# Attention units inside a projection: scores of unit u+2 and context of unit u in one insertion, at uneven pairs

## The chip, the cores and the metric

The kernel runs on one core of a Trainium2 chip. The metric is the device time of one execution in microseconds (us). Kernel before: 1154.33 us, the median of 3 runs (1154.14 to 1155.83).

## What is computed

Two layers of a decoder trunk on 256 tokens of width 1024, all in float32:

```python
for l in range(DEPTH):                      # DEPTH = 2
    x = x + 0.5 * swiglu(rmsnorm(x, ...), ...)          # 1024 -> 2816 -> 1024
    h = rmsnorm(x, mix_norm[l])
    proj = h @ w_in                         # q, k, v of A, B, C and 3 x 1024 gate columns
    ya = moba_attention(qa, ka, va) @ w_branch_a                 # A: causal, 4 heads of 64
    yb = sliding_window_sink_attention(qb, kb, vb, sinks) @ w_branch_b   # B: window 128, sink
    oc = differential_attention(q1, q2, k1, k2, vc, lam)         # (A1 - lam * A2) V, 4 heads
    yc = from_heads(rmsnorm(oc, diff_subln) * (1 - lam_init)) @ w_branch_c
    x = x + (sigmoid(g0) * ya + sigmoid(g1) * yb + sigmoid(g2) * yc) @ w_out
    x = x + 0.5 * swiglu(rmsnorm(x, ...), ...)
```

Every q and k head is normalised and rotated (rope) first. With 256 tokens A is plain causal attention.

## The kernel before

**Engines.** Each engine runs a list of its own, in the order in which the Python code emits it, and they meet through counting semaphores (`sem[...]`). TensorE (PE) multiplies. A float32 weight is split into two parts: ScalarE (ACT) writes `w_high` (`high`, L846), VectorE (DVE) writes the rest `w_low` (`low`, L1089). A product is three passes (`three_passes`, L489, L492, L493). Weights pass through a ring of 6 slots in units called pairs: one pair is 12 matmuls of 128x512, and ACT and DVE prepare pair m+5 or so while PE runs pair m.

**The mixing stage** of a layer is the projection `h @ w_in` in 46 pairs (`PROJ`: QC, KC, VC, QA, VA with four pairs each, KBC with two, then six gate chunks with four each), then 8 pairs for the three branch products and 8 for `w_out`. The attention is put in between these pairs. It consists of 8 units (`UNITS`: 0 to 3 of kind C, 4 and 5 of A, 6 and 7 of B), two heads each, and a unit u takes, in this order:

- S: its scores on PE (`scores`, L693, L694, banks 4 and 5), then `mask_scores` on DVE (L1261 to L1274) and `exps` on ACT (L994), then `normalise` on DVE (L1289 to L1305)
- T: the probabilities are turned on PE (`turn_probs`, L708; three transposes for C, six for A and B), and copied by ACT (`copy_probs`, L1003)
- C: the context product on PE (`context`, L718 to L725), read by ACT (`read_context`, L1011, L1014) and for A and B also by DVE (`context_low`, L1312), which alone counts `context_read` there

In the kernel before, unit u has S ahead of pair 16+3u, T four pairs behind S and C five behind S. The rotated q and k are turned by PE in four rope turns (`rope_turn`, L678; ahead of pairs 10, 15, 25, 31) and copied by ACT (`copy_rope`, L985). The four contexts of C are squared (`SUBLN_AT`, ACT L1043), summed (DVE L1319), turned into a scale (POOL) and scaled (`subln`, DVE L1328), and then turned by PE ahead of pair 37 (`O_TURN`, L503). Turned rope blocks, probabilities, contexts and these last blocks share banks 6 and 7, which is why PE waits for their readers.

What belongs to PE's insertion ahead of pair p stands in the lists of ACT and DVE at step m = p + 5 (RING - 1), and exps and normalise at p + 6, each ahead of the `high` or `low` of that step. `read_proj` (L961) empties a chunk's bank at the step six behind its last pair. Four gate chunks are copied and get their sigmoid later, at steps 44 to 47 (`SIGMOID_AT`, L1050); all others at once. Behind the projection the B branch is multiplied first, then A (`a_quarter`, banks 0 to 3), then C.

Of the kernel before, what the change touches and what calls it, by code (L numbers as in the profile page):

```python
# [41 lines left out]
P = 128  # L42
# [17 lines left out]
PROJ = [(QC, 512), (KC, 512), (VC, 512), (QA, 512), (VA, 512), (KBC, 256)] + [(GATES + 512 * g, 512) for g in range(6)]  # L60
# [36 lines left out]

TURN_AFTER, CONTEXT_AFTER = 4, 5

# [8 lines left out]
    "proj_done": len(PROJ), "proj_read": len(PROJ), "head_squares": 5, "head_totals": 6, "heads_scaled": 6, "tables_ready": 1, "rope_done": 5,  # L108
# [35 lines left out]
def build(nc, a):  # L144
    ctx = ExitStack()
    with ctx:
# [75 lines left out]
        GROUP_BANKS = {ST_FFN1: (4, 5, 6, 7), ST_MIX: (2, 3, 2, 3), ST_O: (6, 7, 6, 7), ST_MERGED: (2, 3, 2, 3), ST_FFN2: (4, 5, 6, 7)}  # L222
# [19 lines left out]
        def a_quarter(half, cols):  # L242
            return bank[half + 2 * cols]
# [23 lines left out]
        def _(sp):  # L267
# [79 lines left out]
            for layer in range(DEPTH):  # L347
# [10 lines left out]
                fill(layer, n, local_heads(a["w_branch_b"], layer))  # L358
                n += 1
                for w, k0 in ((a["w_branch_a"], 0), (a["w_branch_c"], 0), (a["w_branch_c"], 2),  # L360
                              (a["w_out"], 0), (a["w_out"], 2), (a["w_out"], 4), (a["w_out"], 6)):
# [13 lines left out]
        ROPE_CHUNKS = {0: 1, 1: 2, 3: 3, 4: 4, 5: 5}  # L375
        SQUARES_AT = {0: 9, 1: 13, 3: 21, 4: 28, 5: 32}
        ROPE_AT = {0: 10, 1: 14, 3: 22, 4: 29, 5: 33}
        SIGMOID_AT = {6: 44, 7: 45, 8: 46, 9: 47}
        SUBLN_AT = 35
        LAMBDA_AT = 15  # L380
        MERGE_B_AT, MERGE_A_AT, MERGE_C_AT, MERGED_AT = 52, 54, 55, (56, 60)

        ROPE_HEADS = {0: (0, 8, 0, [(0, 8, True)]), 1: (1, 8, 8, [(1, 8, False)]), 3: (0, 8, 16, [(2, 4, True), (3, 4, False)]),
                      4: (1, 4, 24, [(4, 4, True)]), 5: (0, 2, 28, [(5, 2, False)])}
# [14 lines left out]
        def _(pool):  # L399
# [47 lines left out]
            def scale_context(layer):  # L447

                total, v, r = (small[:, k, 0:HALVES * 4] for k in (4, 2, 7))
                pool.wait_ge(sem["head_totals"], value("head_totals", layer, 6))  # L450
# [34 lines left out]
        def _(pe):  # L485
# [181 lines left out]
            def rope_turn(layer, n):  # L667

                first, count, _ = ROPE_TURNS[n]
                pe.wait_ge(sem["rope_done"], value("rope_done", layer, (1, 2, 3, 5)[n]))  # L670
# [11 lines left out]
            def scores(layer, u):  # L682

                kind, qb, kb, _ = UNITS[u]
# [12 lines left out]
            def turn_probs(layer, u):  # L697
# [7 lines left out]
                pe.wait_ge(sem["rope_copied"], value("rope_copied", layer, sum(pos < UNITS[u][3] + TURN_AFTER for _, _, pos in ROPE_TURNS)))  # L705
                for t in range(1 if kind == "C" else 2):
                    for b in range(3):
                        last = nc.tensor.transpose(bank[6 + t][:, b * P:(b + 1) * P], probs_of[u % 2][:, t, b * P:(b + 1) * P], ident[:, :])  # L708
                last.then_inc(sem["probs_turned"], 1)

            def context(layer, u):

                kind = UNITS[u][0]
                pe.wait_ge(sem["probs_copied"], value("probs_copied", layer, u + 1))
                if kind == "C":
                    out, c0 = bank[7], 384 + u * P
# [4 lines left out]
                else:  # L721
                    for half, queries, keys in ((0, slice(0, S), slice(0, S)), (1, slice(P, S), slice(S, S + P))):
                        for t in range(2):
                            c0 = (2 * (u - 4) + t) * DH if kind == "A" else 256 + t * DH
                            last = nc.tensor.matmul(bank[6][t * DH:t * DH + DH, queries], values[:, half, c0:c0 + DH], probsT[:, t, keys],  # L725
# [3 lines left out]
            def mixing(layer):  # L729
                chunk, j = 0, 0  # L730
                for m in range(PROJ_PAIRS):
# [20 lines left out]
                    if m == O_TURN:  # L752
                        pe.wait_ge(sem["subln_ready"], value("subln_ready", layer, 1))
                        pe.wait_ge(sem["context_read"], value("context_read", layer, 6))
# [11 lines left out]
            def branches(layer):  # L766
                p = BRANCH0

                pe.wait_ge(sem["scores_masked"], value("scores_masked", layer, 8))
                pe.wait_ge(sem["context_read"], value("context_read", layer, 8))  # L770
                last_pairs(layer, p, oT_high, oT_low, 2, True, release=1)

                pe.wait_ge(sem["proj_read"], value("proj_read", layer, len(PROJ)))
                last_pairs(layer, p + 2, oT_high, oT_low, 0, True, release=2, banks=a_quarter)
# [58 lines left out]
        def _(act):  # L833
# [113 lines left out]
            def read_proj(layer, chunk):  # L947
# [5 lines left out]
                done = {3: 1, 4: 2, 5: 3}.get(chunk)  # L953
# [3 lines left out]
                for half in range(HALVES):  # L957
                    source, scale = bank[2 * (chunk % 2) + half], norm_scale[:, half:half + 1]
                    if chunk >= 6:
                        c0 = 512 * (chunk - 6)  # L960
# [5 lines left out]
                             5: [(qk_raw[0], 0, 0, 128), (values, 256, 128, 128)]}[chunk]  # L966
# [4 lines left out]
            def head_squares(layer, chunk):  # L971
# [3 lines left out]
                if chunk:  # L975
                    act.wait_ge(sem["rope_done"], value("rope_done", layer, {1: 1, 3: 2, 4: 3, 5: 4}[chunk]))
# [23 lines left out]
            def copy_probs(layer, u):  # L1000
                act.wait_ge(sem["probs_turned"], value("probs_turned", layer, u + 1))
                for t in range(1 if UNITS[u][0] == "C" else 2):
                    last = act.activation(probsT[:, t], bank[6 + t][:, 0:3 * P], ACT.Copy)  # L1003
# [449 lines left out]
```

## Time and profile before

| | |
|---|---|
| median of 3 runs | 1154.33 us |
| the profiled execution | 1154.52 us, its span 1152.7 us |
| PE busy | 1141.2 us (99%) |
| DVE busy | 781.1 us (68%) |
| ACT busy | 639.1 us (55%) |
| granted TensorE clock | 1.0 throughout |

How to read it: the span runs from the first to the last instruction, and the execution's own time is 1.8 us more. PE's records overlap, since matmuls are pipelined, so a matmul of 0.39 us is followed by the next one 0.23 us later; costs on PE are read from start to start. ACT and DVE records overlap too, by some 0.1 us.

### The profile page before, as it was taken

The page shows a single profiled execution, that of the slowest core. Times are in us where ns is not written, and L with a number is a line of the kernel's source. Part 1 is how long each engine was busy: PE and PEld are TensorE (multiplying, and loading weights), DVE is VectorE, ACT ScalarE, POOL GpSimd, SP SyncE. Part 2 cuts the span into 40 slices and gives each one's busy share as a digit, 9 for nine tenths or more (in the row PEclk, how much of TensorE's full clock was granted, in tenths as well). Part 3 has the DMA queues.
Part 4 walks back from the last instruction along what each step waited for, and adds up shares of the span by engine and source line. Part 5 has one row for each costly group of instructions (what it writes and reads, how often), then busy time and mean ns, then how long its engine had stood idle before and what let it go on. Part 6 is the DMA issues. An engine that isn't in the chain of part 4 may idle for free.

```text
span 1152.7 us, 16118 instructions
## 1 busy us (share of the span) xinstructions
PE 1141.2 (99%) x5963; PEld 961.8 (83%) x5963; DVE 781.1 (68%) x1072; ACT 639.1 (55%) x936; POOL 71.5 (6%) x81
## 2 busy tenths in 40 slices
PE   7999999999999999999999999999999999999998
PEld 6888888888778888888888888888887788888887
DVE  4766657778857676566677656668687495766655
ACT  6555545657773565455555545556576745555542
POOL 3100000221100000000040000002110000000000
PEclk9999999999999999999999999999999999999999
DMA  9956554544534665555566555536445445655620
GB/s 311 290 189 199 194 186 146 164 166 147 169 135 172 219 204 193 188 184 193 175 161 232 194 188 186 190 103 215 146 151 179 174 141 191 225 184 188 197 89 37
DMA packets 138364, 207.34 MB, mean 180 GB/s; under 512 B 6818, under 2 KB 99028, under 8 KB 138292
## 3 DMA queue, kind: packets, MB, share of 16 engines
q1 hardware_dynamic: 137444, 205.55, 54.0%
q0 software_dynamic: 752, 0.79, 0.8%
q8 instruction: 47, 0.77, 0.3%
q14 instruction: 25, 0.20, 0.0%
q10 hardware_dynamic: 96, 0.02, 0.0%
HBM read 205.29 MB, written 1.05 MB: 179 GB/s over the span
## 4 chain that ended last, share of the span: by engine, by line
PE 95%; DVE 1%; ACT 1%; DMA 1%; issue 0%; SPq 0%; DVEq 0%; ACTq 0%
PE bank L521 27%; PE bank L489 17%; PE bank L493 16%; PE bank L492 16%; PE bank L525 14%; PE bank L503 1%; DMA raw<-in_ffn_w_up 1%; PE bank L708 1%; PE bank L678 1%; PE bank L694 1%; PE bank L693 1%; PE bank L725 1%; DVE probs L1261 0%; DVE work L1125 0%; DVE oT_low L1100 0%
## 5 line engine op out<-in xcount | busy, mean ns | idle before, releaser
L1089 DVE TENSOR_TENSOR w_low<-raw,w_high 128x1024 fp32r<-128x1024 f32 x388 | 471.9, 1234 | 291.4 <-ACT w_high L846 291.1
L846 ACT ACTIVATE w_high<-raw 128x1024 fp32r<-128x1024 f32 x388 | 402.7, 1056 | 328.8 <-PE bank L489 112.6
L521 PE MATMUL bank<-xT,w_high 128*128 128x512 f32 x1392 | 342.1, 391 | 2.5 <-DVE work L1123 1.9
L521 PEld LDWEIGHTS bank<-xT,w_high 128*128 128x128 f32 x1392 | 254.5, 188 | 54.6 <-DVE work L1131 2.2
L525 PEld LDWEIGHTS bank<-xT,w_low 128*128 128x128 f32 x1408 | 181.2, 191 | 7.6 <-issue 0.6
L525 PE MATMUL bank<-xT,w_low 128*128 128x256 f32 x1408 | 185.0, 283 | 0.4 <-DVE w_low L1089 0.4
L489 PE MATMUL bank<-w_high,xT 128*128 128x512 f32 (+1 forms) x448 | 177.1, 395 | 0.1
L493 PE MATMUL bank<-w_low,xT 128*128 128x512 f32 (+1 forms) x448 | 171.6, 383 | 0.0
L492 PE MATMUL bank<-w_high,xT 128*128 128x512 f32 (+1 forms) x448 | 171.4, 383 | 0.0
L489 PE MATMUL bank<-w_high,oT_high 128*128 128x512 f32 x416 | 162.3, 390 | 0.0
L493 PE MATMUL bank<-w_low,oT_high 128*128 128x512 f32 x416 | 161.9, 389 | 0.0
L492 PE MATMUL bank<-w_high,oT_low 128*128 128x512 f32 x416 | 161.9, 389 | 0.0
L489 PEld LDWEIGHTS bank<-w_high,xT 128*128 128x128 f32 x448 | 84.3, 188 | 20.2 <-issue 5.6
L493 PEld LDWEIGHTS bank<-w_low,xT 128*128 128x128 f32 x448 | 84.2, 188 | 17.0
L492 PEld LDWEIGHTS bank<-w_high,xT 128*128 128x128 f32 x448 | 84.4, 188 | 14.7
L493 PEld LDWEIGHTS bank<-w_low,oT_high 128*128 128x128 f32 x416 | 78.1, 188 | 16.3
L492 PEld LDWEIGHTS bank<-w_high,oT_low 128*128 128x128 f32 x416 | 78.1, 188 | 16.1
L489 PEld LDWEIGHTS bank<-w_high,oT_high 128*128 128x128 f32 x416 | 78.1, 188 | 16.0
L908 ACT ACTIVATE work<-work 128x512 f32<-128x512 f32 x44 | 27.9, 634 | 67.5 <-DVE work L1125 67.5
L426 POOL TENSOR_SCALAR small<-small 128x2 f32<-128x2 f32 x6 | 1.2, 192 | 714.7 <-ACT scratch L883 714.7
L994 ACT ACTIVATE probs<-probs,stats 128x128 f32<-128x128 f32 x64 | 28.4, 449 | 14.4 <-DVE stats L1274 14.4
L1123 DVE TENSOR_TENSOR work<-bank,work 128x512 f32<-128x512 f32 x44 | 30.1, 685 | 8.7 <-ACT work L901 8.3
(129 smaller groups left out, 746.7 us busy)
## 6 DMA issues: line engine op xcount, KB each, us to landing
raw<-in_w_in SPq DMA_DIRECT2D x92, 512.0 KB, 4.5
raw<-in_ffn_w_down SPq DMA_DIRECT2D x88, 512.0 KB, 4.2
raw<-in_ffn_w_gate SPq DMA_DIRECT2D x87, 512.0 KB, 4.0
raw<-in_ffn_w_up SPq DMA_DIRECT2D x87, 512.0 KB, 4.9
raw<-in_w_out SPq DMA_DIRECT2D x16, 512.0 KB, 4.5
raw<-in_w_branch_c SPq DMA_DIRECT2D x8, 512.0 KB, 4.2
raw<-in_w_branch_b SPq DMA_DIRECT2D x4, 512.0 KB, 6.4
raw<-in_w_branch_a SPq DMA_DIRECT2D x4, 512.0 KB, 4.7
```

The costliest lines, as they stand in the source:

```text
L489: first = nc.tensor.matmul(out, left_high, w_high[:, slot, cols], start=start, stop=False)
L492: nc.tensor.matmul(out, left_low, w_high[:, slot, cols], start=False, stop=False)
L493: return nc.tensor.matmul(out, left_high, w_low[:, slot, cols], start=False, stop=stop)
L503: last = nc.tensor.transpose(bank[GROUP_BANKS[stage][2 * group + n // 2]][:, (n % 2) * S + half * P:(n % 2) * S + half * P + P], source[:, ...
L521: return nc.tensor.matmul(bank[n][:, :], w_high[:, slot, column(k, n)], xT[:, k], start=k == 0, stop=k == KB - 1)
L525: return nc.tensor.matmul(bank[n][:, 0:S], weights[:, slot, column(k, n)], xT_high[:, k], start=start, stop=False)
L678: last = nc.tensor.transpose(bank[6 + b // 2][:, (b % 2) * S + half * P:(b % 2) * S + half * P + P], roped[:, half, (b + (n == 3)) * P:(b ...
L846: act.activation(w_high[:, slot], raw[:, in_slot, (p % 2) * 1024:(p % 2) * 1024 + 1024], ACT.Copy).then_inc(sem["high_ready"], 1)
L908: act.activation(silu[:, :, :], gate_scaled[:, :, :], ACT.Silu).then_inc(sem["silu_ready"], 1)
L994: last = act.activation(probs[:, t, cols], probs[:, t, cols], ACT.Exp, bias=neg_max[:, n:n + 1], accum_out=row_sum[:, n:n + 1])
L1089: dve.tensor_tensor(w_low[:, slot], raw[:, FILL_SLOT[p // 2], (p % 2) * 1024:(p % 2) * 1024 + 1024], w_high[:, slot].bitcast(F32), ALU.sub ...
L1123: dve.tensor_tensor(gate_scaled[:, :, :], banks[:, 0:2, 0:S], gate_scaled[:, :, :], ALU.add).then_inc(sem["gate_summed"], 1)
```

## The change

- **Places.** A table `SLOTS` gives ten uneven places. S of unit u stands at `SLOTS[u]`, and in the same insertion, right behind it, C of unit u-2. T of unit u stands one pair behind `SLOTS[u+1]`. So S is ahead of pairs 16, 20, 24, 27, 30, 33, 36, 39; T ahead of 21, 25, 28, 31, 34, 37, 40, 43; C ahead of 24, 27, 30, 33, 36, 39, 42, 45. Rope turns are ahead of 10, 15, 26, 35, O_TURN ahead of 43, SUBLN_AT is 39.
- **Banks.** The context has half a bank of its own (bank 7, columns 256 to 511). Turned probabilities take bank 6 and, with six blocks, the first half of bank 7. The C kind no longer waits for the context before it. The O blocks take banks 4 and 5.
- **Rotations.** The rope work of chunks 4 and 5 is one piece (step 31).
- **Normalising C.** `normalise` scales one product less; the copy of the context in ACT applies the rest as a scale, in two activations (128x128) in place of one.
- **Branches.** A is multiplied first, then B in banks 0 to 3, and gate chunks come in the order 0, 1, 2, 4, 3, 5. `SIGMOID_AT` stays at steps 44 to 47.

```diff
+GATE_ORDER = (0, 1, 2, 4, 3, 5)
-UNITS = [("C", h, 4 + h, 16 + 3 * h) for h in range(4)] + [("A", 8 + j, 10 + j, 28 + 3 * j) for j in range(2)] \
-    + [("B", 12 + j, 14, 34 + 3 * j) for j in range(2)]
-ROPE_TURNS = [(0, 4, 10), (4, 4, 15), (8, 4, 25), (12, 3, 31)]
-O_TURN = 37
-TURN_AFTER, CONTEXT_AFTER = 4, 5
+SLOTS = [16, 20, 24, 27, 30, 33, 36, 39, 42, 45]
+ROPE_TURNS = [(0, 4, 10), (4, 4, 15), (8, 4, 26), (12, 3, 35)]
+O_TURN = 43
+TURN_LATER = 1
-        SUBLN_AT = 35
+        SUBLN_AT = 39
...
             def rope_turn(layer, n):
-                    pe.wait_ge(sem["context_read"], value("context_read", layer, {2: 2, 3: 4}[n]))
+                    pe.wait_ge(sem["probs_copied"], value("probs_copied", layer, {2: 2, 3: 5}[n]))
+                    pe.wait_ge(sem["context_read"], value("context_read", layer, {2: 1, 3: 4}[n]))
...
             def turn_probs(layer, u):
                 pe.wait_ge(sem["probs_ready"], value("probs_ready", layer, u + 1))
-                if u > 0:
-                    pe.wait_ge(sem["context_read"], value("context_read", layer, u))
-                if u == 6:
-                    pe.wait_ge(sem["blocks_low"], value("blocks_low", layer, banks_split(ST_O, 0, 1)))
+                if kind != "C":
+                    pe.wait_ge(sem["context_read"], value("context_read", layer, u))
...
-                    for u, (_, _, _, pos) in enumerate(UNITS):
-                        if m == pos:
-                            scores(layer, u)
-                    for u, (_, _, _, pos) in enumerate(UNITS):
-                        if m == pos + TURN_AFTER:
-                            turn_probs(layer, u)
-                        if m == pos + CONTEXT_AFTER:
-                            context(layer, u)
+                    if m in SLOTS[:8]:
+                        scores(layer, SLOTS.index(m))
+                    if m in SLOTS[2:]:
+                        context(layer, SLOTS.index(m) - 2)
+                    if m - TURN_LATER in SLOTS[1:9]:
+                        turn_probs(layer, SLOTS.index(m - TURN_LATER) - 1)
...
-                    act.activation(o_nat[:, :, c0:c0 + P], bank[7][:, 0:S].rearrange("p (t c) -> p t c", t=2), ACT.Copy
-                                   ).then_inc(sem["context_read"], 1)
+                    for half in range(HALVES):
+                        last = act.activation(o_nat[:, half, c0:c0 + P], bank[7][:, S + half * P:S + half * P + P], ACT.Copy,
+                                              scale=inv_sum_of[u % 2][:, half:half + 1])
+                    last.then_inc(sem["context_read"], 1)
...
+                    if m - (RING - 1) in SLOTS[2:]:
+                        read_context(layer, SLOTS.index(m - (RING - 1)) - 2)
+                    if m - RING in SLOTS[:8]:
+                        exps(layer, SLOTS.index(m - RING))
+                    if m - RING + 1 - TURN_LATER in SLOTS[1:9]:
+                        copy_probs(layer, SLOTS.index(m - RING + 1 - TURN_LATER) - 1)
...
-                    dve.tensor_scalar(inv_sum[:, 2:4], inv_sum[:, 2:4], neg_lam[:, 0:1], None, ALU.mult)
-                        dve.tensor_scalar(probs[:, 1, cols], probs[:, 1, cols], inv_sum[:, 2 + half:3 + half], None, ALU.mult)
+                    dve.scalar_tensor_tensor(ratio[:, 0:2], inv_sum[:, 2:4], neg_lam[:, 0:1], row_sum[:, 0:2], ALU.mult, ALU.mult)
```

The order of instructions, which the tables set, is shown at three places. First ACT near the end of the projection, from step 44 before: the context of unit 6 read (L1014), the four late sigmoids (L1050) with the `high` of each step (L846) between them, and the copy of the last unit's turned probabilities (L1003).

```order
L1014 ACTIVATE oT_high<-bank 128x256
L1050 ACT_TABLE_LOAD
L1050 ACTIVATE gates<-gates 128x2x512
L846 ACTIVATE w_high<-raw 128x1024
L1050 ACTIVATE gates<-gates 128x2x512
L846 ACTIVATE w_high<-raw 128x1024
L1003 ACTIVATE probsT<-bank 128x384 x2
L1050 ACTIVATE gates<-gates 128x2x512
L846 ACTIVATE w_high<-raw 128x1024
L961 ACTIVATE gates<-bank,small 128x512 x2
L1014 ACTIVATE oT_high<-bank 128x256
L1050 ACTIVATE gates<-gates 128x2x512
```

And now, from step 44 too, where it is the context of unit 5 that is read (lines of the changed kernel: read_context L1028, sigmoid L1063, `high` L857, exps L1005 with the sink's L1008, copy_probs L1015, read_proj L972).

```order
L1028 ACTIVATE oT_high<-bank 128x256
L1063 ACT_TABLE_LOAD
L1063 ACTIVATE gates<-gates 128x2x512
L857 ACTIVATE w_high<-raw 128x1024
L1005 ACT_TABLE_LOAD
L1005 ACTIVATE probs,stats<-probs,stats 128x128
...
L1008 ACTIVATE stats<-stats 128x4
L1015 ACTIVATE probsT<-bank 128x256
L1015 ACTIVATE probsT<-bank 128x512
L1063 ACT_TABLE_LOAD
L1063 ACTIVATE gates<-gates 128x2x512
L857 ACTIVATE w_high<-raw 128x1024
```

The exps of unit 7 have moved in between the first and the second sigmoid, and two table loads stand there that were not there before.

Second, DVE where the contexts of C are summed and scaled, before: sum (L1319), scaling (L1328), context_low of unit 4 (L1312) and the mask of unit 6 (from L1261).

```order
L1319 TENSOR_REDUCE small<-scratch 128x8 [waits subln_squares]
L1089 TENSOR_TENSOR w_low<-raw,w_high 128x1024 [waits high_ready]
...
L1305 TENSOR_SCALAR probs<-probs,stats 128x256
L1328 TENSOR_TENSOR o_nat<-o_nat,small 128x2x512 [waits heads_scaled]
L1089 TENSOR_TENSOR w_low<-raw,w_high 128x1024 [waits high_ready]
L1312 TENSOR_TENSOR oT_low<-bank,oT_high 128x256 [waits context_high]
L1089 TENSOR_TENSOR w_low<-raw,w_high 128x1024 [waits high_ready]
L1261 ISA probs,stats<-bank,masks,head_scale 128x128 [waits scores_done,probs_turned]
...
L1274 TENSOR_SCALAR stats<-stats 128x4
```

And now (sum L1330, mask of unit 6 from L1276 to L1289, scaling L1339, context_low of unit 4 L1323).

```order
L1330 TENSOR_REDUCE small<-scratch 128x8 [waits subln_squares]
L1102 TENSOR_TENSOR w_low<-raw,w_high 128x1024 [waits high_ready]
L1276 ISA probs,stats<-bank,masks,head_scale 128x128 [waits scores_done,probs_turned]
...
L1287 TENSOR_SCALAR stats<-stats,params 128x2 x2
L1289 TENSOR_SCALAR stats<-stats 128x4
L1339 TENSOR_TENSOR o_nat<-o_nat,small 128x2x512 [waits heads_scaled]
L1323 TENSOR_TENSOR oT_low<-bank,oT_high 128x256 [waits context_high]
L1102 TENSOR_TENSOR w_low<-raw,w_high 128x1024 [waits high_ready]
```

The mask of unit 6 and the scaling now stand between the `low` of step 40 and context_low of unit 4.

Third, PE around the fourth rope turn, before: S of unit 5 (L693, L694), the rope turn (L678), T of unit 4 (L708) and C of unit 4 (L725), with the pairs between them left out.

```order
L693 MATMUL bank<-gates 128x128
L694 MATMUL bank<-gates 128x256
L678 MATMUL bank<-ident,o_nat 128x128 [waits context_read,rope_copied,rope_done]
L678 MATMUL bank<-ident,o_nat 128x128 x5
...
L708 MATMUL bank<-ident,probs 128x128 [waits rope_copied,context_read,probs_ready]
L708 MATMUL bank<-ident,probs 128x128 x5
...
L725 MATMUL bank<-probsT,values 64x256 [waits probs_copied]
...
L725 MATMUL bank<-probsT,values 64x128 x2
```

And now (T of unit 4 L708, rope turn L679, S of unit 6 L694 and L695, C of unit 4 L729, T of unit 5 L708 at the end).

```order
L708 MATMUL bank<-ident,probs 128x128 [waits rope_copied,context_read,probs_ready]
L708 MATMUL bank<-ident,probs 128x128 x5
...
L679 MATMUL bank<-ident,o_nat 128x128 [waits probs_copied,context_read,rope_copied,rope_done]
L679 MATMUL bank<-ident,o_nat 128x128 x5
...
L694 MATMUL bank<-gates 128x128 [waits scores_masked,rope_copied]
L695 MATMUL bank<-gates 128x256
...
L729 MATMUL bank<-probsT,values 64x256 [waits rope_copied,context_read,probs_copied]
...
L729 MATMUL bank<-probsT,values 64x128 x2
...
L708 MATMUL bank<-ident,probs 128x128 [waits rope_copied,context_read,probs_ready]
```

The rope turn now follows T of unit 4 by one pair and waits for its copy, and T of unit 5 follows C of unit 4 by one pair.

## Rows read from the trace of the kernel before

**Rows 1.** Page, part 1: busy time and share of the span.

```profile
PE 1141.2 (99%) x5963; PEld 961.8 (83%) x5963; DVE 781.1 (68%) x1072; ACT 639.1 (55%) x936; POOL 71.5 (6%) x81
```

**Rows 2.** Waits of PE: who it waited for, us in total, times, longest.

```profile
PE bank L708 <- DVE oT_low L1100: 0.8, 2, 0.4
PE bank L718 <- ACT probsT L1003: 0.6, 2, 0.3
```

**Rows 3.** PE timeline, 301 to 326 us: start, us, operation, idle before.

```profile
301.29 0.40 PE L493 MATMUL bank<-w_low,xT 128*128 128x512 f32 x1
...
302.10 0.47 PE L489 MATMUL bank<-w_high,xT 128*128 128x512 f32 x1
302.41 0.39 PE L492 MATMUL bank<-w_high,xT 128*128 128x512 f32 x1
...
304.70 0.39 PE L493 MATMUL bank<-w_low,xT 128*128 128x512 f32 x1
...
305.82 0.50 PE L489 MATMUL bank<-w_high,xT 128*128 128x512 f32 x1
...
324.12 0.39 PE L493 MATMUL bank<-w_low,xT 128*128 128x512 f32 x1
...
325.53 0.48 PE L489 MATMUL bank<-w_high,xT 128*128 128x512 f32 x1
```

**Rows 4.** PE timeline around S of units 4 and 5.

```profile
286.52 0.39 PE L493 MATMUL bank<-w_low,xT 128*128 128x512 f32 x1
...
287.70 0.50 PE L489 MATMUL bank<-w_high,xT 128*128 128x512 f32 x1
...
296.86 0.39 PE L493 MATMUL bank<-w_low,xT 128*128 128x512 f32 x1
...
298.67 0.47 PE L489 MATMUL bank<-w_high,xT 128*128 128x512 f32 x1
```

**Rows 5.** ACT timeline, 294 to 299 us.

```profile
294.75 1.24 ACT L961 ACTIVATE gates<-bank,small 128x512 f32<-128x512 f32 x2
295.89 0.37 ACT L1011 ACTIVATE o_nat<-bank 128x256 f32<-128x256 f32 x1
297.15 1.06 ACT L1043 ACTIVATE scratch<-o_nat 128x1024 f32<-128x1024 f32 x1 [0.89 <-DVE o_nat L1241]
298.12 1.05 ACT L846 ACTIVATE w_high<-raw 128x1024 fp32r<-128x1024 f32 x1
```

**Rows 6.** ACT timeline, 325 to 333 us.

```profile
325.81 0.88 ACT L1003 ACTIVATE probsT<-bank 128x384 f32<-128x384 f32 x2
326.57 0.40 ACT L994 ACTIVATE probs<-probs,stats 128x128 f32<-128x128 f32 x1
...
328.42 1.06 ACT L846 ACTIVATE w_high<-raw 128x1024 fp32r<-128x1024 f32 x1
329.37 0.38 ACT L1014 ACTIVATE oT_high<-bank 128x256 fp32r<-128x256 f32 x1
329.81 1.28 ACT L1050 ACT_TABLE_LOAD   x1
331.11 1.06 ACT L1050 ACTIVATE gates<-gates 128x1024 f32<-128x1024 f32 x1
332.07 1.05 ACT L846 ACTIVATE w_high<-raw 128x1024 fp32r<-128x1024 f32 x1
```

**Rows 7.** DVE timeline, 306 to 313 us.

```profile
306.21 1.22 DVE L1328 TENSOR_TENSOR o_nat<-o_nat,small 128x1024 f32<-128x1024 f32 x1
307.35 1.22 DVE L1089 TENSOR_TENSOR w_low<-raw,w_high 128x1024 fp32r<-128x1024 f32 x1
308.49 0.42 DVE L1312 TENSOR_TENSOR oT_low<-bank,oT_high 128x256 fp32r<-128x256 f32 x1
...
309.98 0.35 DVE L1261 CUSTOM_DVE_ANT_0 probs<-bank,masks,head_scale 128x128 f32<-128x128 f32 x1
...
312.27 1.22 DVE L1089 TENSOR_TENSOR w_low<-raw,w_high 128x1024 fp32r<-128x1024 f32 x1
```

More of the change, by code:

```diff
@@ L714, in context @@
                 pe.wait_ge(sem["probs_copied"], value("probs_copied", layer, u + 1))
+                if u > 0:
+                    pe.wait_ge(sem["context_read"], value("context_read", layer, u))
+                pe.wait_ge(sem["rope_copied"], value("rope_copied", layer, sum(pos < SLOTS[u + 2] for _, _, pos in ROPE_TURNS)))
+                out = bank[7][:, S:2 * S]
                 if kind == "C":
-                    out, c0 = bank[7], 384 + u * P
+                    c0 = 384 + u * P
                     pT, v = probsT[:, 0], values[:, :, c0:c0 + P]
@@ L724, in context @@
                             c0 = (2 * (u - 4) + t) * DH if kind == "A" else 256 + t * DH
-                            last = nc.tensor.matmul(bank[6][t * DH:t * DH + DH, queries], values[:, half, c0:c0 + DH], probsT[:, t, keys],
+                            last = nc.tensor.matmul(out[t * DH:t * DH + DH, queries], values[:, half, c0:c0 + DH], probsT[:, t, keys],
                                                     start=half == 0, stop=half == 1)
@@ L753, in mixing @@
                         pe.wait_ge(sem["subln_ready"], value("subln_ready", layer, 1))
-                        pe.wait_ge(sem["context_read"], value("context_read", layer, 6))
+                        pe.wait_ge(sem["scores_masked"], value("scores_masked", layer, 8))
                         turn_group(layer, ST_O, 0, o_nat)
@@ L952, in read_proj @@
                     act.wait_ge(sem["norm_ready"], value("norm_ready", layer, 2))
-                done = {3: 1, 4: 2, 5: 3}.get(chunk)
+                done = {3: 1, 4: 2}.get(chunk)
                 if done:
@@ L1001, in copy_probs @@
                 act.wait_ge(sem["probs_turned"], value("probs_turned", layer, u + 1))
-                for t in range(1 if UNITS[u][0] == "C" else 2):
-                    last = act.activation(probsT[:, t], bank[6 + t][:, 0:3 * P], ACT.Copy)
+                flat = probsT[:, :, :].rearrange("p t k -> p (t k)")
+                for first, b, width in ((0, 6, 3 * P),) if UNITS[u][0] == "C" else ((2 * S, 7, S), (0, 6, 2 * S)):
+                    last = act.activation(flat[:, first:first + width], bank[b][:, 0:width], ACT.Copy)
                 last.then_inc(sem["probs_copied"], 1)
@@ L1361, in mixing @@
                 for m in range(4, FFN2_0 - MIX0 + 4):
-                    for u, (_, _, _, pos) in enumerate(UNITS):
-                        if m == pos + 6:
-                            normalise(layer, u)
-                    for u, (_, _, _, pos) in enumerate(UNITS):
-                        if m == pos + 5:
-                            mask_scores(layer, u)
+                    if m - RING in SLOTS[:8]:
+                        normalise(layer, SLOTS.index(m - RING))
+                    if m - (RING - 1) in SLOTS[:8]:
+                        mask_scores(layer, SLOTS.index(m - (RING - 1)))
                     for chunk, at in ROPE_AT.items():
@@ L1378, in mixing @@
                         blocks_low(layer, ST_O, 0, G_SUBLN)
-                    for u, (kind, _, _, pos) in enumerate(UNITS):
-                        if m == pos + CONTEXT_AFTER + RING - 1 and kind != "C":
-                            context_low(layer, u)
-                    if m == MERGE_B_AT:
+                    if m - (RING - 1) in SLOTS[6:]:
+                        context_low(layer, SLOTS.index(m - (RING - 1)) - 2)
+                    if m == MERGE_A_AT:
                         dve.wait_ge(sem["proj_read"], value("proj_read", layer, len(PROJ)))
                         for n in range(4):
+                            merge_a(layer, n)
+                    if m == MERGE_B_AT:
+                        for n in range(4):
                             merge_b(layer, n)
-                    if m == MERGE_A_AT:
-                        for n in range(4):
-                            merge_a(layer, n)
                         for n in range(2):
```

105 lines of the change are left out of this document (53 added, 52 removed).

## The prediction

> **What bounds the kernel now.** I read the page first, then PE's waits, then the timelines of PE, ACT and DVE in the mixing stage of the first layer. PE is busy for 99% of the span [rows 1], so only two things on PE can move the end: the work in its own list, and waits. In the stage that is changed, the list of PE's waits holds two entries, each met twice, once per layer: the turn of probabilities waits for DVE (0.4 us at most), and the first context waits for ACT's copy (0.3 us) [rows 2]. The other engines have spare time on average (DVE 68%, ACT 55%) [rows 1], but the average hides what matters: whether ACT and DVE answer within the pair or two that PE leaves them.
>
> Prices on PE are read from the last matmul ahead of an insertion to the first one behind it, less the usual step, which is 0.23 us (302.41 to 304.70 are ten steps) [rows 3]. T with six transposes costs 301.29 to 302.10, so 0.58. C of kind A costs 304.70 to 305.82, so 0.89. T of unit 6 costs 324.12 to 325.53, so 1.18: 0.60 of it is the wait that the list gives as 0.4 [rows 2, 3], so a wait costs some 0.2 more than its idle time. S alone costs 286.52 to 287.70, so 0.95; S of unit 5 with six transposes right behind it 296.86 to 298.67, so 1.58 [rows 4]. The first step behind an insertion is 0.31 in place of 0.23 [rows 3], so a pair with an insertion ahead of it lasts 2.83 (302.10 to 304.70 and one step) and a plain one some 2.74.
>
> **What the change takes off PE, per layer.**
>
> - The wait of T of unit 6 for the O blocks' readers: these blocks go to banks 4 and 5 now. 0.60.
> - The wait of the first context: T of unit 0 is ahead of pair 21 and its context ahead of 24, three pairs for one copy. Idle 0.3 and the 0.2 on top: 0.47.
> - Fewer insertions. Before there are 26 places (24 for the units, rope turns 10 and 15; the two others and O share a place with an S). Now there are 22: 10 slots, 8 turns (one shared with O), 4 rope turns of their own. Each place fewer saves a first step's 0.08; that two kinds of work stand together gives nothing more (1.58 against 0.95 + 0.58) [rows 3, 4]. S with a context behind it does not occur in this trace. Its nearest row is S with transposes, which gives nothing or 0.05 lost; what C of kind A pays beyond its eight passes cannot be over 0.2, so six such pairs of work give between 0 and 1.2 per layer. I take 0.07 for each of the four places, 0.3, since that is the nearer row.
>
> Sum: 0.60 + 0.47 + 0.30 = 1.37 per layer, 2.7 in both. The bounds are 2.1 (merging gives nothing) and 4.6.
>
> **What it takes off or puts on ACT and DVE.** `normalise` of C loses one scaling of three blocks on DVE, and the context copy becomes two activations on ACT. Both stand in steps of units 0 to 3, where PE leaves two or three pairs between T and C, and as many until the next C asks for the last one's reading. I cost them at nothing, hidden under the pairs; without that cover the second activation would be at most 0.4 in four places. The joined rope piece has its turn nine pairs later. A first and B second swaps two products of equal size, whose first quarters wait for the O blocks, turned three pairs earlier: nothing. The gate order only keeps the later reads of q and k safe, but it leaves the sigmoids at steps 44 to 47, and that is not nothing (below). The DMA queue follows `low`, and PE never waits for a weight in this stage; a microsecond's delay there is hidden by a ring of five pairs.
>
> **What is late next.** I count each chain from a fixed point on PE, ACT and DVE by their timelines, start to start where something follows. Durations: two activations that empty a bank 1.14 (294.75 to 295.89), squares of the contexts 0.97 (297.15 to 298.12) [rows 5]; copy of six turned blocks 0.76, exps of kind B 1.85 (326.57 to 328.42), one `high` 0.95, context read 0.38, table load 1.30, sigmoid 0.96; handing from PE to ACT 0.28 (PE goes on at 325.53, the copy starts at 325.81) [rows 3, 6]; DVE's scaling 1.14, `low` 1.14, rest of a context 0.42, mask of kind B 2.29 (309.98 to 312.27) [rows 7]. A handing back I take as 0.1 to 0.2.
>
> 1. *Fourth rope turn, ahead of pair 35.* It now waits for the copy of unit 4's probabilities, turned one pair before. In ACT's list that copy stands behind a gate chunk's reading and the exps of unit 5. From the end of pair 33: ACT 0.28 + 1.14 + 1.75 (exps of kind A, without the sink's) + 0.76 + 0.1 = 4.03; PE 0.58 + 2.83 = 3.41. Wait 0.6. On PE everything is queued behind it.
> 2. *T of unit 5, ahead of pair 37.* It waits for `context_read` of unit 4, whose product is ahead of pair 36, and that is counted by DVE after mask of unit 6 and the scaling of C. Still from the end of pair 33: ACT ends its copy at 3.9, the squares at 4.9, `high` at 5.85; DVE then `low` 7.0, sum of squares 8.1 (as a `low`), `low` 9.3. S of unit 6 ends at 4.03 + 0.58 + 2.83 + 0.95 = 8.4, so DVE is the later one. It ends mask, scaling and rest at 9.3 + 2.29 + 1.14 + 0.42 = 13.15, with handing 13.35. PE is there at 8.4 + 0.89 + 2.83 = 12.1. Wait 1.2. With DVE free when S ends it would still be 0.28 + 2.29 + 1.14 + 0.42 + 0.2 - 3.72 = 0.6; with yet another `low` in the way 2.4.
> 3. *T of unit 7, ahead of pair 43.* It waits for the context of unit 6, product ahead of pair 42. ACT's list from the end of C of unit 5 (ahead of pair 39): 0.28, context read 0.38, table load and sigmoid 2.26, high 0.95, **table load and exps of unit 7** 3.15, copy of unit 6's probabilities 0.76, **table load and sigmoid** 2.26, high 0.95, sigmoid 0.96, high 0.95, reading a gate chunk 1.14, context read 0.38, handing 0.1, DVE's rest 0.42, handing 0.2: 15.1. PE: pairs 39, 40 and 42 at 2.83, pair 41 at 2.74, T 0.58, C 0.89: 12.7. Wait 2.4. Before, the last exps come ahead of the first sigmoid and one load is enough; now exps stand between two sigmoids, which costs two loads more, 2.6 us, on the one engine whose answer PE needs.
>
> For these loads the Trainium skill has a rule that speaks against the change ("ScalarE: Activation LUTs", section "What ACT_TABLE_LOAD costs"): a change of set costs the load of 1283 ns and a drain of some 1380 ns besides. Here the load is 1.28, and it starts 0.06 behind the end of the activation before it and ends 0.02 ahead of the next [rows 6]: the trace agrees with the load and shows no such drain. By that rule the three loads would add 4.1 per layer and the time would be some 1168.
>
> Sum per layer: 0.6 + 1.2 + 2.4 = 4.2 put on, 1.37 taken off, 2.85 net; 5.7 in both layers, as both have the same lists. The profiled execution takes 1154.52 (span 1152.7 and 1.8 around it), so 1160.2; it lies 0.2 above the median, so the median becomes 1160.0.
>
> **Rivals.**
>
> - *More waits follow* (0.17). T of unit 6 waits for the context of unit 5: DVE 0.28 + 2.29 + 0.42 + 0.2 = 3.2 against PE's 3.7, margin 0.5. S of unit 6 waits for the fourth rope turn's copy, margin 0.7 (PE 3.41 after the turn starts; squares, `high` and a copy of 0.8 on ACT 2.7). If both slip by one activation, 1.5 more per layer, 1163. Against it: both margins are counted with the handing.
> - *Only the table loads bite* (0.13). If ACT and DVE run further ahead than I count, the first two waits vanish, and 2.4 - 1.37 = 1.1 per layer is left: 1156.5. For it: before, ACT sits idle for 0.9 ahead of the squares [rows 5].
> - *It does what it says, faster* (0.06). All three chains fit. The third decides: it must shrink from 15.1 to 12.7, which is 2.4, almost exactly the two loads; ACT would have to hide them. Then 1154.33 - 2.7 = 1151.6. Against it: an engine's list is run in order, and the load stands in the row as 1.28 us of ACT's own time [rows 6].
> - *A load empties the engine* (0.02), by which every load costs more than its row. By the rows alone that is at most one activation's overlap of 0.1 each, which changes nothing; by the figure of the Trainium skill above it is 1168.
>
> **The numbers.** The forecast, three waits, has 0.62: 1160.0, its own range 1157.5 to 1162. The range that should hold 8 of 10 goes down to the table loads alone and up to the further waits: 1156.8 to 1163. A measurement of this kernel tells 0.2% (2.3 us) from nothing. Slower: 0.62 + 0.17 + 0.02, less a tail: 0.80. Within 0.2%: the loads alone (1156.5 lies just inside), and a small forecast: 0.14. Faster: 0.06.
>
> **What would show it.** In the profile after: the two waits of rows 2 are gone; PE has three new ones per layer, at the rope turn for the copy of probabilities (0.4 to 0.9), at T for the rest of a context on DVE twice (1.0 to 1.6, and 2.0 to 2.8 near the end of the projection). ACT shows 5.1 us more of table loads, four loads more at the exps and sigmoid lines. I am wrong if PE is idle for less than 2 us per layer there, if a chain's end is set by another engine than named, or if S with a context behind it costs much less than 1.8.

## The result, and the profile after

| | before | after |
|---|---|---|
| median of the runs | 1154.40 us (1154.14 to 1155.83, 4 runs) | 1164.26 us (1163.03 to 1164.57, 4 runs) |
| ratio | | 1.0081, 95% interval 1.0069 to 1.0093 |
| profiled execution | 1154.52 us, span 1152.7 | 1163.03 us, span 1161.2 |

The change costs 9.9 us. The forecast was 1160.0, with a range up to 1163.0: right in sign, too small by 4.3.

The page's row for PE of the changed kernel looks like [rows 1]: the loss is under one per cent, so it has to be looked for in waits.

```profile
PE 1142.4 (98%) x5963; PEld 962.9 (83%) x5963; DVE 777.3 (67%) x1054; ACT 644.1 (55%) x946; POOL 68.3 (6%) x79
```

PE's waits in the changed stage (engine, line, whom it waited for: total us, times, longest). L708 is T, L679 a rope turn; "issue" means that the list names no releaser, and the timelines further down do.

```profile
PE bank L708 <- issue: 6.9, 4, 2.4
...
PE bank L679 <- ACT probsT L1015: 1.9, 4, 0.7
```

Both entries of [rows 2] are gone. In their place PE idles 8.8 us in eight waits, four per layer, where three were forecast. The same timeline as [rows 3, 4], of the changed kernel's first layer (start us, us, engine line operation tile, and in brackets the idle time and its releaser): the third rope turn, the fourth, T of unit 5, S of unit 7 with C of unit 5 behind it, and T of unit 7 with the O blocks.

```profile
276.59 0.39 PE L493 MATMUL bank<-w_low,xT 128*128 128x512 f32 x1
277.29 1.06 PE L679 MATMUL bank<-ident,o_nat 128*128 128x128 f32 x8 [0.31 <-ACT probsT L1015]
278.11 0.47 PE L489 MATMUL bank<-w_high,xT 128*128 128x512 f32 x1
...
309.25 0.39 PE L493 MATMUL bank<-w_low,xT 128*128 128x512 f32 x1
310.29 0.85 PE L679 MATMUL bank<-ident,o_nat 128*128 128x128 f32 x6 [0.65 <-ACT probsT L1015]
310.89 0.48 PE L489 MATMUL bank<-w_high,xT 128*128 128x512 f32 x1
...
318.08 0.39 PE L493 MATMUL bank<-w_low,xT 128*128 128x512 f32 x1
319.49 0.85 PE L708 MATMUL bank<-ident,probs 128*128 128x128 f32 x6 [1.02 <-issue]
320.09 0.48 PE L489 MATMUL bank<-w_high,xT 128*128 128x512 f32 x1
...
325.40 0.39 PE L493 MATMUL bank<-w_low,xT 128*128 128x512 f32 x1
325.72 0.50 PE L694 MATMUL bank<-gates 64*128 64x128 f32 x4
...
326.58 0.87 PE L729 MATMUL bank<-probsT,values 128*64 128x256 f32 x8
327.39 0.50 PE L489 MATMUL bank<-w_high,xT 128*128 128x512 f32 x1
...
339.91 0.39 PE L493 MATMUL bank<-w_low,xT 128*128 128x512 f32 x1
342.71 0.85 PE L708 MATMUL bank<-ident,probs 128*128 128x128 f32 x6 [2.41 <-issue]
343.39 1.04 PE L503 MATMUL bank<-ident,o_nat 128*128 128x128 f32 x8
344.18 0.47 PE L489 MATMUL bank<-w_high,xT 128*128 128x512 f32 x1
```

Priced as in the prediction (last matmul ahead to first behind, less a step of 0.23), with the same insertion unhindered beside it:

| insertion | gap | alone | wait's cost | forecast |
|---|---|---|---|---|
| third rope turn | 1.29 | 0.79 | 0.50 | none |
| fourth rope turn | 1.41 | 0.57 | 0.84 | 0.6 |
| T of unit 5 | 1.78 | 0.57 | 1.21 | 1.2 |
| T of unit 7 and O | 4.04 | 1.45 | 2.59 | 2.4 |

The "alone" values are the gaps of the same work unhindered: both rope turns in experiment 4, T of unit 4 in this kernel, T with the O blocks in experiment 6. S with C of kind A costs 1.76 (325.40 to 327.39 less 0.23), against 0.95 + 0.89 apart in [rows 3, 4]. The prediction had taken 1.8 for such a pair, and "much less" did not come.

Waits and places together come to 3.5 per layer: all gaps and slow first steps of the first layer's mixing stage behind its first rope turn sum to 27.94 in 21 places after, and to 24.42 in 25 places before. Two layers make 7.0, and 2.9 of the 9.9 is missing. It is in PE's granted clock, as experiment 2 shows. The windows show (from:to, length, then busy us of PE, PEld, DVE, ACT and POOL, then the granted clock of PE, DMA share and GB/s) the stretch behind the longest wait in the first layer, then ahead of and behind the same wait in the second:

```profile
342.00:345.00 3.00, 2.29 (x18) 2.19 (x19) 1.15 (x2) 2.92 (x6) 0.00 (x0) 1.00 0.76 306
912.00:915.00 3.00, 0.59 (x4) 0.19 (x3) 1.71 (x3) 2.92 (x5) 0.00 (x0) 1.00 0.41 157
915.00:918.00 3.00, 3.00 (x15) 3.00 (x15) 1.33 (x2) 2.86 (x5) 0.00 (x0) 0.50 0.47 193
918.00:921.00 3.00, 3.00 (x13) 2.44 (x13) 2.62 (x3) 1.64 (x2) 0.00 (x0) 0.93 0.78 221
```

In the second layer the clock falls to 0.50, the 1.2 GHz level, right behind 2.41 us of idle PE; in the first layer, behind an idle time of the same length, it does not. The timeline there:

```profile
914.87 1.41 PE L708 MATMUL bank<-ident,probs 128*128 128x128 f32 x6 [2.41 <-issue]
916.07 1.91 PE L503 MATMUL bank<-ident,o_nat 128*128 128x128 f32 x8
```

T lasts 1.41 in place of 0.85, the O blocks 1.91 in place of 1.04, and the mixing stage's gaps sum to 29.59 in this layer against 27.94 in the first: 1.65 for one fall. The other three runs have a mean clock of 0.997 against this one's 0.998 and lie 1.1 to 1.5 above it, which fits one more fall each.

### The profile page after: what moved, and what is told of

Its sections match the earlier page's. It is cut to its first block, busy times and chain, and to the rows that moved or that the text cites. A ratio compares the mean times of both kernels' runs of the same rounds, so it can differ in the third digit from the quotient of the medians.

```text
span 1161.2 us, 16104 instructions
## 1 busy us (share of the span) xinstructions
PE 1142.4 (98%) x5963; PEld 962.9 (83%) x5963; DVE 777.3 (67%) x1054; ACT 644.1 (55%) x946; POOL 68.3 (6%) x79
## 4 chain that ended last, share of the span: by engine, by line
PE 90%; ACT 3%; DVE 2%; issue 2%; DVEq 1%; DMA 1%; ACTq 0%; SPq 0%
PE bank L521 26%; PE bank L489 15%; PE bank L493 15%; PE bank L492 15%; PE bank L525 14%; PE bank L503 1%; ACT probs L1005 1%; ACT w_high L857 1%; DMA raw<-in_ffn_w_up 1%; PE bank L679 1%; PE bank L708 1%; PE bank L729 1%; PE bank L695 0%; PE bank L694 0%; DVE probs L1276 0%
## 5 line engine op out<-in xcount | busy, mean ns | idle before, releaser
L857 ACT ACTIVATE w_high<-raw 128x1024 fp32r<-128x1024 f32 x388 | 402.1, 1055 | 323.2 <-PE bank L489 112.2
L1005 ACT ACTIVATE probs<-probs,stats 128x128 f32<-128x128 f32 x64 | 28.3, 444 | 22.5 <-DVE stats L1289 22.4
```

Source lines behind the costliest of these rows:

```text
L857: act.activation(w_high[:, slot], raw[:, in_slot, (p % 2) * 1024:(p % 2) * 1024 + 1024], ACT.Copy).then_inc(sem["high_ready"], 1)
L1005: last = act.activation(probs[:, t, cols], probs[:, t, cols], ACT.Exp, bias=neg_max[:, n:n + 1], accum_out=row_sum[:, n:n + 1])
```

## The experiments

All times are medians. The kernel before, run beside them on the same chip, took 1154.37 for the first four kernels and 1154.34 for the last three. Beside the changed kernel it took 1154.40, so the changed kernel's 1164.26 is compared with theirs as it stands.

**1. The sigmoids one pair later.** Then the exps of unit 7 stand ahead of the first sigmoid again, and two table loads per layer go.

```diff
-        SIGMOID_AT = {6: 44, 7: 45, 8: 46, 9: 47}
+        SIGMOID_AT = {6: 45, 7: 46, 8: 47, 9: 48}
```

> The changed kernel with its four late sigmoids one step later (45 to 48), so that all of them come behind the exps of unit 7 and two table loads per layer go (2.6 us of ACT). Theory (the wait of T of unit 7 is ACT's chain with the loads in it, and the fall of TensorE's granted clock to 0.5 behind it is a consequence of that 2.4 us of idle PE): the wait goes in both layers (2.6 each by start to start), granted clock 1.0 throughout, 1164.3 - 5.3 - some 3 for the clock = 1155.5 to 1156.5. Rival 1 (the clock falls for another reason, say the denser insertions): the clock still falls and the time is 1158.5 to 1159.5. Rival 2 (the wait is the one pair of distance between product and turn, loads or not): no change beyond 1 us. The waits at the fourth rope turn and at T of unit 5 stay (0.65 and 1.02 us idle).

Measured 1156.56 (1155.69 to 1158.08), ratio 1.0019 (1.0009 to 1.0029). PE's waits at T in this kernel, and on PE's timeline the last matmul ahead of T of unit 7 and T itself:

```profile
PE bank L708 <- issue: 2.0, 2, 1.0
```

```profile
340.40 0.39 PE L493 MATMUL bank<-w_low,xT 128*128 128x512 f32 x1
340.63 0.82 PE L708 MATMUL bank<-ident,probs 128*128 128x128 f32 x6
```

T of unit 7 starts one step behind the last matmul, so the longest wait is gone. That is worth 7.7 us: 2 x 2.59 of waiting, and 2.5 that no term of the wait explains. But the edit takes more than the two loads out of ACT's way. These are its readings of the contexts of units 5 and 6 in this kernel:

```profile
327.99 0.39 ACT L1028 ACTIVATE oT_high<-bank 128x256 fp32r<-128x256 f32 x1 [2.18 <-PE bank L729]
...
339.02 0.38 ACT L1028 ACTIVATE oT_high<-bank 128x256 fp32r<-128x256 f32 x1
```

They are 11.03 apart, and 14.27 in the changed kernel (327.50 and 341.77, further down): 3.24 less. Besides the loads one sigmoid (0.96) has moved behind the second reading, and ACT idles 0.48 of the gain away ahead of the exps. The two loads alone are 2.60, just the length of the wait (2.59). That they alone would have been enough is worked out from the rows and was not run.

T of unit 5 still waits 1.0 per layer, and so do the rope turns (2.0 in four waits, 0.7 at most). The time is 0.1 above the range that I had expected. Two of the ten runs, 1157.86 and 1158.08, have a mean clock of 0.999. They were not profiled, so where the clock fell in them is not known; the longest wait is not needed for it.

**2. The same wait, filled.** Nine products of zeros run ahead of T of unit 7, started by a signal that has come by then. PE still can't go on before ACT and DVE answer.

```diff
+                    if m == SLOTS[8] + TURN_LATER:
+                        pe.wait_ge(sem["scores_masked"], value("scores_masked", layer, 8))
+                        for _ in range(9):
+                            nc.tensor.matmul(bank[5][:, :].rearrange("p (a b) -> p a b", a=4), zero[:, :],
+                                             zero[:, :].unsqueeze(1).to_broadcast([P, 4, P]), start=True, stop=True)
```

> The changed kernel with nine matmuls of zeros (128x512, about 0.23 us each, 2.1 us in all) on PE ahead of T of unit 7, into a bank that is free there; nothing else is touched, so T still starts when ACT and DVE have done with the context. Theory (idle PE of 2.4 us makes the clock fall): the wait is filled, granted clock 1.0 in both layers, and the time falls by what the clock costs, 2.5 to 3.5 us, to 1161 to 1162. Rival (the clock falls for another reason): no change, 1164.3, or up to 0.5 more.

Measured 1161.41 (1161.25 to 1161.78), ratio 1.0062 (1.0045 to 1.0078), clock 1.0 in all four runs. PE at T of unit 7:

```profile
339.99 0.39 PE L493 MATMUL bank<-w_low,xT 128*128 128x512 f32 x1
340.22 2.20 PE L752 MATMUL bank<-zero 128*128 128x512 f32 x9
342.80 0.85 PE L708 MATMUL bank<-ident,probs 128*128 128x128 f32 x6 [0.38 <-issue]
...
344.28 0.48 PE L489 MATMUL bank<-w_high,xT 128*128 128x512 f32 x1
```

From 339.99 to 344.28 the gap is 4.06, where it was 4.04: the wait is as long as ever, only PE isn't idle in it. The time falls by 2.85 all the same. So 2.85 us of the change's 9.9 are the clock, and 1161.41 less 1154.37, 7.04, is what the waits and places make: twice the 3.52 of the gaps.

**3. The `low` of a context first.** On DVE, context_low stands ahead of the sum over blocks and of the scaling of C.

```diff
+                    if m - (RING - 1) in SLOTS[6:]:
+                        context_low(layer, SLOTS.index(m - (RING - 1)) - 2)
...
-                    if m - (RING - 1) in SLOTS[6:]:
-                        context_low(layer, SLOTS.index(m - (RING - 1)) - 2)
```

> The changed kernel with DVE's rest of a context ahead of the sum and the scaling of the contexts of C in its list, so that T of unit 5 no longer waits for the scaling (1.14 us). Theory (that wait is DVE's list): its idle time falls from 1.02 us to at most 0.1, 1.1 to 1.2 us less per layer, 1162.0; T of unit 7 waits 2.4 as before, since its chain begins behind it. Rival (another chain, ACT's reading of the context or the mask, ends within a few tenths behind it): less than 0.6 per layer, 1163 or more.

Measured 1160.49 (1159.11 to 1162.87), ratio 1.0049 (1.0032 to 1.0066). On PE's timeline T of unit 5, which has no idle time now, and then the two windows behind T of unit 7 in this kernel's profiled execution:

```profile
318.93 0.85 PE L708 MATMUL bank<-ident,probs 128*128 128x128 f32 x6
```

```profile
342.00:345.00 3.00, 2.83 (x15) 2.86 (x16) 1.30 (x2) 3.00 (x5) 0.00 (x0) 0.57 0.58 236
915.00:918.00 3.00, 3.00 (x18) 2.71 (x16) 1.62 (x2) 3.00 (x6) 0.00 (x0) 0.64 0.45 182
```

The wait of T of unit 5 is down to a gap of 0.65, as expected. The four runs are 1162.87, 1160.86, 1160.12 and 1159.11 at mean clocks of 0.997, 0.998, 0.999 and 1.0. The first shows falls in both layers. The last agrees with the sum without the clock (1161.41 less 2 x 1.13 is 1159.15). The kernel is the same in all four, so behind the same wait the clock falls in some executions and not in others. I had expected 1162.0, which is the price with a fall in each layer.

**4. The copy of turned probabilities first.** For units 0 to 4, ACT copies them ahead of the exps of its step.

```diff
+                    if m - RING + 1 - TURN_LATER in SLOTS[1:6]:
+                        copy_probs(layer, SLOTS.index(m - RING + 1 - TURN_LATER) - 1)
...
-                    if m - RING + 1 - TURN_LATER in SLOTS[1:9]:
+                    if m - RING + 1 - TURN_LATER in SLOTS[6:9]:
```

> The changed kernel with ACT's copy of turned probabilities ahead of the exps in the same step, for units 0 to 4 (as in the kernel before). Theory (waits in a row absorb each other): the waits of the third (0.31 us idle) and fourth rope turn (0.65) for that copy go; the first is a gain of 0.5 per layer, the second is given back, because T of unit 5 then waits longer by the same 0.6 to 0.8 for a DVE chain that does not start at the rope turn. So T of unit 5 idles 1.7 to 1.9 and the time is 1163.3 (1.0 less). Rival (each wait is a cost of its own): 1161.6 (2.7 less), T of unit 5 idles 1.0 as before.

Measured 1162.94 (1162.15 to 1163.77), ratio 1.0072 (1.0055 to 1.0089). The third rope turn and T of unit 5:

```profile
277.09 1.03 PE L679 MATMUL bank<-ident,o_nat 128*128 128x128 f32 x8
...
319.24 0.85 PE L708 MATMUL bank<-ident,probs 128*128 128x128 f32 x6 [1.85 <-issue]
```

Both rope turns run unhindered (gaps 0.79 and 0.57), but T of unit 5 idles 1.85 in place of 1.02. Its wait costs 2.05 (gap 2.62), which is 1.21 plus the 0.84 that the fourth rope turn no longer waits. The wait was passed on: T of unit 5 still waits for a chain of ACT and DVE that, counted from the third rope turn, ends no earlier. Only the 0.5 of the third rope turn is a gain, 1.0 in both layers, and 1164.26 less 1162.94 is 1.3.

**5. The first and the third together**, sigmoids later and the `low` of a context first.

```diff
-        SIGMOID_AT = {6: 44, 7: 45, 8: 46, 9: 47}
+        SIGMOID_AT = {6: 45, 7: 46, 8: 47, 9: 48}
...
+                    if m - (RING - 1) in SLOTS[6:]:
+                        context_low(layer, SLOTS.index(m - (RING - 1)) - 2)
...
-                    if m - (RING - 1) in SLOTS[6:]:
-                        context_low(layer, SLOTS.index(m - (RING - 1)) - 2)
```

> The changed kernel with the sigmoids one pair later (two table loads fewer per layer) and, on DVE, the `low` of a context ahead of the sum over blocks and its rest. Nothing else. My theory (the waits are separate terms, each with its own mender): from the 1156.56 of the first of these edits alone, the wait of T of unit 5, 1.2 per layer, goes as well and nothing takes its place; 1154.0 to 1154.5, the same as the kernel before. The two rope turns still wait (0.5 and 0.8 by the gaps), the clock stays at 1.0. Rival (the edits mend the same time twice): 1155.5 to 1156.5.

Measured 1154.09 (1153.26 to 1155.44, 10 runs), ratio 0.9998 (0.9988 to 1.0007). The terms add up: 1156.56 less 2 x 1.13 is 1154.3. Three of its ten runs are at 1155.23 to 1155.44 with a mean clock of 0.998 or 0.999; the other seven are at 1.0 and at most 1154.28. The profiled one is of these, and its windows tell where:

```profile
24.00:27.00 3.00, 1.48 (x6) 0.96 (x6) 2.81 (x5) 1.50 (x3) 1.95 (x4) 1.00 1.11 323
27.00:30.00 3.00, 3.00 (x13) 2.66 (x13) 2.75 (x4) 3.00 (x4) 0.00 (x0) 0.53 1.12 217
```

The clock falls here at 27 us, far from the change, behind a wait of 1.40 us for DVE that every one of these kernels has near 25 us, and that no fall follows in the other eight profiles. Of the 27 runs of the kernel before beside it, two are at 0.998 and 1155.9.

**6. All three edits**, with the sum of squares of the contexts one step later.

```diff
-        SIGMOID_AT = {6: 44, 7: 45, 8: 46, 9: 47}
-        SUBLN_AT = 39
+        SIGMOID_AT = {6: 45, 7: 46, 8: 47, 9: 48}
+        SUBLN_AT = 40
...
+                    if m - RING + 1 - TURN_LATER in SLOTS[1:6]:
+                        copy_probs(layer, SLOTS.index(m - RING + 1 - TURN_LATER) - 1)
...
-                    if m - RING + 1 - TURN_LATER in SLOTS[1:9]:
+                    if m - RING + 1 - TURN_LATER in SLOTS[6:9]:
...
+                    if m - (RING - 1) in SLOTS[6:]:
+                        context_low(layer, SLOTS.index(m - (RING - 1)) - 2)
...
-                    if m - (RING - 1) in SLOTS[6:]:
-                        context_low(layer, SLOTS.index(m - (RING - 1)) - 2)
```

> All three menders together: the sigmoids one pair later (and the sum of squares of the contexts one step later), the `low` of a context ahead of the sum over blocks, and the copy of turned probabilities ahead of the exps for units 0 to 4. My theory: what the change takes off PE (the two old waits and fewer insertions) is real and was only hidden by four new waits per layer. With those gone the rope turns cost 0.8 and 0.6, T of unit 5 idles at most 0.3 and T of unit 7 not at all, the clock stays at 1.0: 1156.56 less 2 x (0.5 + 0.84) less 2 x 1.2 is 1151.5, with a small rest at T of unit 5 1151.4 to 1152.2, faster than the kernel before by 2 to 3. Rival 1 (waits are passed on, as the copy's place alone passed them to T of unit 5): T of unit 5 waits for 1.0 or more, 1153.5 to 1154.5, no faster than before. Rival 2 (the change saves PE nothing by itself): 1154 or more without any wait of these four.

Measured 1151.74 (1151.33 to 1153.16, 11 runs), ratio 0.9977 (0.9968 to 0.9986). It beats both kernels: 2.6 below before, 12.5 below the changed kernel. Of the four waits this is what PE's timeline still shows, at T of unit 5:

```profile
317.10 0.85 PE L708 MATMUL bank<-ident,probs 128*128 128x128 f32 x6 [0.15 <-issue]
```

Its idle time is 0.15 (gap 0.91, 0.34 above unhindered). The stage's gaps sum to 23.17 in a layer, 1.25 less than before, which is 2.5 in both. What the later squares are worth by themselves no run shows. One of the eleven runs, 1153.16, has a mean clock of 0.999; the others are at 1.0.

**7. The kernel before with two more table loads per layer.** Only its first late sigmoid moves, so that exps stand between sigmoids as in the changed kernel.

```diff
-        SIGMOID_AT = {6: 44, 7: 45, 8: 46, 9: 47}
+        SIGMOID_AT = {6: 42, 7: 45, 8: 46, 9: 47}
```

> The kernel before with one number changed: the first sigmoid two steps earlier, so that the exps of unit 7 stand between two sigmoids, as in the changed kernel: two table loads more per layer, four in all, 5.2 us more on ACT. My theory (a load costs only where PE asks for ACT's answer inside it): in the kernel before PE leaves that much between T and C of the last units, so the loads are hidden: 1154.2 to 1155.0, clock 1.0. Rival (table loads cost their time wherever they stand, or drain the engine): 1157 to 1159.6.

Measured 1154.31 (1154.06 to 1154.59, 10 runs), ratio 0.9999 (0.9990 to 1.0009). ACT's table loads in this stage and the last context behind them:

```profile
322.37 1.28 ACT L1050 ACT_TABLE_LOAD   x1
...
327.61 1.28 ACT L994 ACT_TABLE_LOAD   x1
...
333.10 1.28 ACT L1050 ACT_TABLE_LOAD   x1
...
340.30 0.38 ACT L1014 ACTIVATE oT_high<-bank 128x256 fp32r<-128x256 f32 x1
```

Three loads of 1.28 stand there in place of one, the last context (340.30) follows them, and in this profile's list PE's waits at T and C are those of [rows 2], digit for digit. So two more loads per layer have no price of their own here, and a load costs where PE waits for what is queued behind it.

## Why the prediction was right in sign and too small

*What the change takes off PE* was nearly right, forecast 1.37 per layer. The whole change nets 3.52 per layer and the four waits are 5.14 of the other sign, so 1.62 came off: 0.60 and 0.57 for the two old waits (the second gap was 1.15 against 0.58), and the rest, 0.45, for the places. Experiment 6 shows it net: 1.25 and the 0.34 still waited.

*Fourth rope turn*, forecast 0.6, measured 0.84. ACT's order was as counted: the exps of unit 5 (from 307.43) are ahead of the copy.

```profile
307.43 0.40 ACT L1005 ACTIVATE probs<-probs,stats 128x128 f32<-128x128 f32 x1
...
309.18 0.85 ACT L1015 ACTIVATE probsT<-bank 128x256 f32<-128x256 f32 x2
```

The copy ends at 310.03, and PE starts at 310.29: handing back takes 0.26, where I took 0.1.

*T of unit 5*, forecast 1.2, measured 1.21, and by the engine named. DVE's timeline has mask, scaling and context_low in that order; the last ends at 319.39 and T starts at 319.49.

```profile
315.56 0.34 DVE L1276 CUSTOM_DVE_ANT_0 probs<-bank,masks,head_scale 128x128 f32<-128x128 f32 x1
...
317.84 1.22 DVE L1339 TENSOR_TENSOR o_nat<-o_nat,small 128x1024 f32<-128x1024 f32 x1
318.97 0.42 DVE L1323 TENSOR_TENSOR oT_low<-bank,oT_high 128x256 fp32r<-128x256 f32 x1
```

*T of unit 7*, forecast 2.4, measured 2.59. ACT's list from the reading of unit 5's context, with its three loads, to the reading of unit 6's:

```profile
327.50 0.39 ACT L1028 ACTIVATE oT_high<-bank 128x256 fp32r<-128x256 f32 x1 [2.18 <-PE bank L729]
327.95 1.28 ACT L1063 ACT_TABLE_LOAD   x1
329.25 1.06 ACT L1063 ACTIVATE gates<-gates 128x1024 f32<-128x1024 f32 x1
...
331.27 1.28 ACT L1005 ACT_TABLE_LOAD   x1
...
335.34 1.28 ACT L1063 ACT_TABLE_LOAD   x1
...
341.77 0.38 ACT L1028 ACTIVATE oT_high<-bank 128x256 fp32r<-128x256 f32 x1
```

From 327.39, where PE goes on behind C of unit 5, to T at 342.71 it is 15.3, counted as 15.1. The table loads at the sigmoids and exps of this stage were forecast as well, four more in all:

```profile
L1063 ACT ACT_TABLE_LOAD x4 | 5.1, 1283 | 0.3
L1005 ACT ACT_TABLE_LOAD x2 | 2.6, 1283 | 0.0
```

The Trainium skill ("ScalarE: Activation LUTs", section "What ACT_TABLE_LOAD costs") gives a drain of some 1380 ns on top of each load. The measurement differs: the load at 327.95 starts 0.06 behind the end of the activation before it, the sigmoid follows 0.02 behind the load's end, and in experiment 7 two more loads per layer cost nothing. The rival "a load empties the engine" was near the measured time (1168 against 1164.3) for a reason that the runs refute.

*The third rope turn* was not counted at all. It waits for the copy of unit 1 through the same new wait as the fourth, one pair behind T, with the exps ahead of the copy on ACT: 0.50, 1.0 in both layers. I had drawn the chain where six blocks are turned and not where three are.

*The step that failed* is the sum, "4.2 put on, 1.37 taken off, 2.85 net; 5.7 in both layers": it takes a wait at its own length, as if PE came back as it had left. It has no term for the clock. The 9.9 measured are 5.7 forecast, 1.0 for the third rope turn, 0.4 for the other terms' sizes (put on 0.44 more in the three forecast waits, taken off 0.25 more, per layer), and 2.85 for the clock, which is two thirds of the miss of 4.3. Experiment 2 shows that size with the wait's length unchanged, and experiment 1 shows both going together. The rows of before could not price a fall, since none was in them, but the prediction could have named it as an open cost behind its longest wait. The rival "more waits follow" gave 1163 for waits that did not come.

What stays open is why one wait of 2.41 us brings a fall and the next does not. In the profiled executions it fell behind 2.41 us in one layer of two here and in both layers of experiments 3 and 4, five times in six, and behind the 1.40 us near 25 us in experiment 5, once in nine. It fell neither behind the 1.85 us of experiment 4, in both layers, nor behind any of the six waits of 1.0 us (T of unit 5 here and in experiments 1 and 2). So a longer wait brings it more often, but no length in these profiles settles it.

## What to carry to other kernels

When a step is moved on the busiest engine, write down for each wait that it has or gets what now stands ahead of its releaser on the other engine, for every instance of a loop and not only for the largest one, and count the handing back too (0.26 from ACT to PE here). A forecast wait in an otherwise full PE stream can cost more than its length: behind the 2.41 us here the granted clock fell in five of six profiled cases, at about 1.6 us each, so give such a wait a term for the clock, with a chance. And before a rearrangement is given up, look for the small orders that make its waits: three edits outside PE's list (with the squares one step later), none of which removes arithmetic, turned 9.9 us slower into 2.6 faster.

## What the runs showed of the hardware

- PE's granted clock falls to the 1.2 GHz level right behind some waits and stays there for about 3 us: 0.50 for 915 to 918, 0.93 for the three after. One fall costs 1.65 us by the stage's gaps in the two layers, and 1.4 to 1.9 by the runs whose time and mean clock fit two (1164.17 to 1164.57 less 1161.41, and 1162.87 less 1159.15 in experiment 3).
- It is a matter of the execution: with one kernel four runs gave 1159.1, 1160.1, 1160.9 and 1162.9. Filling the wait with products of zeros, into a bank whose reading is over, narrowed the four runs to 1161.25 to 1161.78 and took 2.85 us off.
- A wait costs 0.18 to 0.19 more than its listed idle time (0.31 and 0.50, 0.65 and 0.84, 1.02 and 1.21, 2.41 and 2.59), as [rows 2, 3] had it for one of 0.4.
- PE starts 0.25 behind the end of ACT's copy (277.29, 310.29) and 0.10 to 0.11 behind the end of DVE's context_low (319.49, 342.71). I had taken one value, 0.1 to 0.2, for both.
- S with C of kind C right behind it costs 1.64 (269.32 and others), 0.11 more than the two apart (0.95 and 0.58), and S with C of kind A 1.76, 0.08 less than apart. Two kinds of work put together save PE the slow first step, 0.1, and nearly nothing else; with kind C the 0.11 takes even that back.
